# Keys' copies and differences over ten k tiles, the decay's chain in smaller pieces, the gate's two weight halves in one product

## The chip, the cores and the metric

The kernel runs on one core of one Trainium2 chip. The metric is the device time of one execution in microseconds, the median of three runs.

## The reference, cut to what matters

A decoder trunk of two post-norm layers on one sequence of 256 tokens, width 2048, in float32. Layer 0 mixes tokens by windowed attention, layer 1 by forgetting attention; after each comes a gated MLP (5632 wide) with a causal convolution of width 3. The change touches the forgetting attention alone:

```python
def forgetting_attention(x, w_qkvf, f_bias, w_o):
    proj = x @ w_qkvf                      # 2048 -> 3*2048 (q, k, v) and 32 gate columns
    q, k, v = ...                          # 32 heads of 64
    fz = proj[..., 3 * B_DIM:] + f_bias
    cum = jnp.cumsum(jax.nn.log_sigmoid(fz), axis=1)      # the decay, per head
    s = q @ k.T * SCALE + cum[query] - cum[key]           # causal
    return softmax(s) @ v, then @ w_o
```

## The kernel before

**Precision.** TensorE multiplies in a format that holds only part of a float32. Every operand is therefore split in a high half (ACT copies it, which rounds it) and a low half (VectorE subtracts the high half from the original), and every product is three matmuls: high by low, low by high, high by high. Activations stand in `xh` and `xl`, weights in `w_hi` and `w_lo`.

**Chunks and the ring.** A group is a product of all 256 tokens with 512 weight columns, summed over 16 k tiles of 128. Two k tiles of weights (512 KB) are a chunk. Chunks go through a ring of four slots: SyncE loads `raw` when the low half of the chunk four earlier is made (`low_ready`), ACT makes `w_hi` (`L553`) when the chunk four earlier has been used by TensorE (`chunks_used`), VectorE makes `w_lo` (`L848`), TensorE multiplies. ACT works three chunks ahead (`AHEAD`), VectorE two (`LOW_AHEAD`). In ACT's and VectorE's programs the generator `slots` interleaves this with other work: it yields k = 0 to 15, the caller puts its step for that k there, and the split of a chunk follows each even k:

```python
for k in range(nk):
    if k == nk - 2:
        split(b4, loc0 + k // 2 + AHEAD)      # VectorE: LOW_AHEAD
    yield k
    if k % 2 == 0 and k != nk - 2:
        split(b4, loc0 + k // 2 + AHEAD)
```

Each engine carries out its own program strictly in the written order. The same k on two engines doesn't mean the same time: each runs as far ahead as its waits let it.

**The forgetting layer.** `mixer_b` has four turns of three groups (queries, keys, values) for eight heads each, turn 0 written out and turns 1 to 3 as a loop. Queries and keys are computed turned (tokens along the columns), 12 matmuls of 256 columns for each k tile (`L1318`, `L1320`, `L1321`); values straight, 6 matmuls of 512 columns (`L1300` to `L1302`). Results stand in banks of PSUM that must be copied out:

- while the keys group is computed, the queries are copied (`query_high` on ACT, `L609`; `query_low` on VectorE, `L938`), for banks b = 0, 1 and halves of the rows h = 0, 1;
- while the values group is computed, the keys are copied (`key_high` on ACT, `L616`, two copies for each b and h; `key_low` on VectorE, `L949`, two differences for each). ACT raises `k_high` with h = 1 only; VectorE waits for it with h = 0 of the same bank;
- after the values group, VectorE and ACT copy the values (`vv`, `L1157` and `L715`), and TensorE's next group, which writes to the same banks, waits for these copies. In turns 1 to 3 and at the output projection's start ACT loads the table for Exp (`L526`) ahead of its copy.

The queries group of turns 1 to 3 has the attention of the heads before woven into it (`attention_slot`). In turn 0 there is none; there the gate is computed: a narrow product with 32 columns (`L1605` to `L1607`, 48 matmuls) between queries and keys, and then in `decay`, under the keys group, the logarithm of the sigmoid and the running sum (VectorE `L1129` to `L1147`, ACT `L733` Exp and `L736` Ln, each with a table load). TensorE transposes the sum for the queries (`L1615`), and GpSimd writes it to memory and loads it back spread over the partitions, twice 1 MB, to make the bias of eight heads; then it loads two rows of the norm's parameters and scales a piece of the residual with them.

Of the kernel before, what the change touches and what calls it, by code (L numbers as in the profile page):

```python
# [26 lines left out]
P = 128  # L27
# [63 lines left out]

LATE = KT - KT // GROUPS
OUT_DONE = 2 * KT - KT // GROUPS
WOVEN_OUT = [(i, k) for ks in (range(LATE), range(LATE, KT)) for i in range(2) for k in ks]
# [34 lines left out]
def trunk(nc, x, a_w_qkv, a_w_o, a_sinks, rel_bias, b_w_qkvf, b_f_bias, b_w_o,  # L129
          ffn_w_up, ffn_conv_w, ffn_conv_b, ffn_w_down, ln_g, ln_b, out):  # L130
    ctx = ExitStack()
    with ctx:
# [46 lines left out]
        with ExitStack() as mix:  # L179
# [4 lines left out]
            with ExitStack() as gating:  # L184
                wf = sb("wf", [P, KT, HEADS], FP32, gating)
                wf_hi = sb("wf_hi", [P, KT, HEADS], F32R, gating)
                wf_lo = sb("wf_lo", [P, KT, HEADS], F32R, gating)
            bias_hold = sb("bias_hold", [P, HG * SPAN], FP32, mix)
# [332 lines left out]
        def _(act):  # L521
# [186 lines left out]
            def mixer_b():  # L708
                def turn(n, b4, first=False, nk=KT):

                    if not first:
                        load_table(ACT.Exp)
                        act.wait_ge(pv_done, n * HG + (GROUPS - 1) * HG)
                        act.wait_ge(chunks_used, n * (3 * KC) + CH_B)
                        act.activation(vv[:, 1, :], bank(0, 1), ACT.Copy).then_inc(acc_free[0][1], 1)  # L715
                    for k in slots(b4, 0, nk):
                        if first:
                            if k % 2 == 0 and k // 2 + 2 < KC:
                                xt_evacuate(2, 0, 1, k // 2 + 2)
                            if k == 13:  # L720
                                act.wait_ge(wf_in, 32)
                                act.activation(wf_hi[:, :, :], wf[:, :, :], ACT.Copy).then_inc(wf_high, 1)
                            continue
                        attention_slot(k, (n + (GROUPS - 1)) * HG, (n + (GROUPS - 1)) * 2, (n - 1) * 4, False)
                    if nk > KT:
                        return
                    act.wait_ge(chunks_used, n * (3 * KC) + (CH_B + KC))
                    for k in slots(b4, KC):
                        if k < 4:
                            query_high(0, k // 2, k % 2, False)  # L730
                        if first and k == 7:
                            act.wait_ge(decay_abs, 1)
                            act.activation(fs[2][:, :], fs[1][:, :], ACT.Exp).then_inc(decay_exp, 1)  # L733
                        if first and k == 9:
                            act.wait_ge(decay_u, 1)
                            act.activation(fs[4][:, :], fs[3][:, :], ACT.Ln).then_inc(decay_ln, 1)  # L736
                    act.wait_ge(chunks_used, n * (3 * KC) + (CH_B + 2 * KC))
                    for k in slots(b4, 2 * KC):
                        if k < 4:
                            key_high(1, k // 2, k % 2)  # L740

                turn(0, CH_B // 4, first=True)
                with act.Fori(0, GROUPS - 1) as i:
                    own.enter(i, 1)
                    turn(i + 1, i * (3 * KC // 4) + (CH_B + 3 * KC) // 4)
                    own.leave(GROUPS - 1)
                turn(GROUPS, CH_O[1] // 4, nk=2 * KT)
# [85 lines left out]
        def _(dve):  # L833
# [287 lines left out]
            def decay(k):  # L1121
# [3 lines left out]
                z, nabs, e, u, lnu, d, zero, cum, ncum = fs  # L1125
                if k == 3:
                    dve.wait_ge(fz_done, 1)
                    dve.wait_ge(wf_in, 32)
                    own.link(dve.tensor_scalar(z[:, :], ps[0:HEADS, 6, 0:SEQ], fbc[:, 0:1], None, ALU.add))  # L1129
                    dve.scalar_tensor_tensor(nabs[:, :], z[:, :], -1.0, z[:, :], ALU.mult, ALU.min).then_inc(decay_abs, 1)  # L1130
                if k == 7:
                    dve.wait_ge(decay_exp, 1)
# [3 lines left out]
                    own.link(dve.tensor_scalar(zero[:, :], d[:, :], 0.0, None, ALU.is_equal))  # L1136
                    own.link(dve.tensor_tensor(d[:, :], d[:, :], zero[:, :], ALU.add))
                    own.link(dve.reciprocal(d[:, :], d[:, :]))
                    own.link(dve.tensor_tensor(d[:, :], d[:, :], e[:, :], ALU.mult))
                if k == 9:  # L1140
                    dve.wait_ge(decay_ln, 1)
                    own.link(dve.tensor_tensor(lnu[:, :], lnu[:, :], zero[:, :], ALU.add))
                    own.link(dve.tensor_tensor(d[:, :], lnu[:, :], d[:, :], ALU.mult))
                    own.link(dve.scalar_tensor_tensor(z[:, :], z[:, :], 0.0, d[:, :], ALU.min, ALU.subtract))
                    own.link(dve.memset(zero[:, :], 1.0))
                    own.link(dve.tensor_tensor_scan(cum[:, :], zero[:, :], z[:, :], 0.0, ALU.mult, ALU.add))
                    dve.tensor_scalar(ncum[:, :], cum[:, :], -1.0, None, ALU.mult).then_inc(cum_ready, 1)  # L1147
                if k == 13:
                    dve.wait_ge(cum_turned, 1)
                    dve.tensor_copy(cumq[:, :, :], ps[:, 7, 0:MT * HEADS].rearrange("p (m h) -> p m h", m=MT)).then_inc(cumq_ready, 1)  # L1150

            def mixer_b():
                def turn(n, b4, first=False, nk=KT):
# [4 lines left out]
                    for k in slots(b4, 0, nk, after_norm=first):  # L1158
                        if first:
                            xt_next(2, 0, 1, k)  # L1160
                            if k == 13:
                                dve.wait_ge(wf_high, 1)
                                dve.tensor_tensor(wf_lo[:, :, :], wf[:, :, :], wf_hi[:, :, :].bitcast(FP32), ALU.subtract).then_inc(wf_low, 1)
                            continue
# [5 lines left out]
                    for k in slots(b4, KC):  # L1170
                        if k < 4:
                            query_low(0, k // 2, k % 2, False, n * 2 + (2 * GROUPS + k // 2 + 1))
                        if first:
                            decay(k)
                    for k in slots(b4, 2 * KC):
                        if k < 4:
                            key_low(1, k // 2, k % 2, n * 2 + (2 + k // 2 + 1))

# [113 lines left out]
        def _(pe):  # L1292
# [289 lines left out]
            def mixer_b():  # L1582
# [11 lines left out]
                def turn(n, b4, first=False):  # L1594
# [5 lines left out]
                    if first:  # L1600

                        pe.wait_ge(wf_low, 1)
                        o = ps[0:HEADS, 6, 0:SEQ]
                        for k in range(KT):
                            pe.matmul(o, wf_lo[:, k, :], xh[:, k, :], start=(k == 0), stop=False)  # L1605
                            pe.matmul(o, wf_hi[:, k, :], xl[:, k, :], start=False, stop=False)
                            last = pe.matmul(o, wf_hi[:, k, :], xh[:, k, :], start=False, stop=(k == KT - 1))  # L1607
                        last.then_inc(fz_done, 1)
                    if not first:
                        narrow_product()  # L1610
                    for k in turned_group(1, n + t1, b4, KC):
                        if first and k == 12:
                            pe.wait_ge(cum_ready, 1)
# [95 lines left out]
```

## Time and profile before

| | |
|---|---|
| median of three runs | 2172.21 us (2171.49 to 2173.5) |
| the profiled execution | 2171.2 us, span 2169.4 us |
| TensorE matmul busy | 2143.6 us (99%) |
| VectorE busy | 1353.8 us (62%) |
| ACT busy | 1068.0 us (49%) |
| GpSimd busy | 214.8 us (10%) |
| mean granted TensorE clock | 0.999 |

Times in the trace are counted from the span's start. The forgetting layer's projections lie between 1002 and 1325 us. The values group begins at 1137.94 in turn 1. A busy TensorE is not TensorE at its peak, since matmuls are pipelined: the distance between the starts of two matmuls is the pace, and a longer distance is a pause.

### The profile page before, as it was taken

The page shows a single profiled execution, that of the slowest core. Times are in us where ns is not written, and L with a number is a line of the kernel's source. Part 1 is how long each engine was busy: PE and PEld are TensorE (multiplying, and loading weights), DVE is VectorE, ACT ScalarE, POOL GpSimd, SP SyncE. Part 2 cuts the span into 40 slices and gives each one's busy share as a digit, 9 for nine tenths or more (in the row PEclk, how much of TensorE's full clock was granted, in tenths as well). Part 3 has the DMA queues.
Part 4 walks back from the last instruction along what each step waited for, and adds up shares of the span by engine and source line. Part 5 has one row for each costly group of instructions (what it writes and reads, how often), then busy time and mean ns, then how long its engine had stood idle before and what let it go on. Part 6 is the DMA issues. An engine that isn't in the chain of part 4 may idle for free.

```text
span 2169.4 us, 41044 instructions
## 1 busy us (share of the span) xinstructions
PE 2143.6 (99%) x15304; PEld 1995.4 (92%) x15304; DVE 1353.8 (62%) x1865; ACT 1068.0 (49%) x1433; POOL 214.8 (10%) x211
## 2 busy tenths in 40 slices
PE   9999999999999999999899999999999999999998
PEld 8998899999999988888798898889999999988887
DVE  5676676666666644446766666676666666655554
ACT  4655465545555543335545545355555555544432
POOL 2000003210000000000330330002121000000000
PEclk9999999999999999999999999999999999999999
DMA  8554567666666656564655655556676666666663
GB/s 280 152 179 138 175 189 211 204 203 192 194 193 193 192 185 203 192 195 142 199 166 161 205 171 156 176 173 204 203 207 197 192 193 192 193 213 193 193 193 125
DMA packets 206604, 407.69 MB, mean 188 GB/s; under 512 B 12832, under 2 KB 13408, under 8 KB 206400
## 3 DMA queue, kind: packets, MB, share of 16 engines
q1 hardware_dynamic: 199680, 384.35, 58.3%
q0 software_dynamic: 5984, 20.74, 3.1%
q10 hardware_dynamic: 864, 1.57, 0.2%
q8 instruction: 49, 0.80, 0.1%
q14 instruction: 27, 0.22, 0.0%
HBM read 404.44 MB, written 2.18 MB: 187 GB/s over the span
## 4 chain that ended last, share of the span: by engine, by line
PE 93%; DVE 4%; issue 1%; ACT 1%; DMA 1%; DVEq 0%; ACTq 0%; SPq 0%
PE ps L1318 18%; PE ps L1321 18%; PE ps L1320 18%; PE ps L1300 11%; PE ps L1301 11%; PE ps L1302 11%; DVE w_lo L848 1%; PE ps L1505 1%; DMA raw<-in_b_w_qkvf_dram 1%; PE ps L1516 1%; PE ps L1517 1%; PE ps L1515 1%; PE ps L1497 0%; PE ps L1402 0%; DVE cg L903 0%
## 5 line engine op out<-in xcount | busy, mean ns | idle before, releaser
L848 DVE TENSOR_TENSOR w_lo<-raw,w_hi 128x1024 fp32r<-128x1024 f32 x725 | 905.5, 1255 | 599.2 <-ACT w_hi L553 596.3
L553 ACT ACTIVATE w_hi<-raw 128x1024 fp32r<-128x1024 f32 x725 | 768.1, 1060 | 919.0 <-PE ps L1321 492.1
L1318 PE MATMUL ps<-xh,w_lo 128*128 128x256 f32 x3572 | 996.8, 279 | 5.1 <-ACT vv L715 2.6
L1321 PE MATMUL ps<-xh,w_hi 128*128 128x256 f32 x3572 | 988.6, 277 | 0.0
L1320 PE MATMUL ps<-xl,w_hi 128*128 128x256 f32 x3572 | 988.5, 277 | 0.0
L1318 PEld LDWEIGHTS ps<-xh,w_lo 128*128 128x128 f32 x3572 | 672.0, 188 | 8.4 <-DVE xl L899 3.1
L1320 PEld LDWEIGHTS ps<-xl,w_hi 128*128 128x128 f32 x3572 | 671.9, 188 | 0.0
L1321 PEld LDWEIGHTS ps<-xh,w_hi 128*128 128x128 f32 x3572 | 671.8, 188 | 0.0
L1302 PE MATMUL ps<-w_hi,hid_h 128*128 128x512 f32 x704 | 273.9, 389 | 0.0
L1301 PE MATMUL ps<-w_hi,hid_l 128*128 128x512 f32 x704 | 273.9, 389 | 0.0
L1300 PE MATMUL ps<-w_lo,hid_h 128*128 128x512 f32 x704 | 273.9, 389 | 0.0
L1300 PEld LDWEIGHTS ps<-w_lo,hid_h 128*128 128x128 f32 x704 | 132.2, 188 | 27.6
L1301 PEld LDWEIGHTS ps<-w_hi,hid_l 128*128 128x128 f32 x704 | 132.2, 188 | 27.3
L1302 PEld LDWEIGHTS ps<-w_hi,hid_h 128*128 128x128 f32 x704 | 132.2, 188 | 27.2
L462 POOL COPY cw<-convcol 128x16 f32 (+1 forms) x40 | 39.6, 991 | 746.9 <-DVE cu L1193 415.3
L1300 PE MATMUL ps<-w_lo,oh 128*128 128x512 f32 x256 | 101.7, 397 | 0.0
L1302 PE MATMUL ps<-w_hi,oh 128*128 128x512 f32 x256 | 99.8, 390 | 0.0
L1301 PE MATMUL ps<-w_hi,ol 128*128 128x512 f32 x256 | 99.8, 390 | 0.0
L1193 DVE SCALAR_TENSOR_TENSOR cu<-ps,cw,cu 128x254 f32<-128x254 f32 (+1 forms) x176 | 76.6, 477 | 1.6
L1193 DVE SCALAR_TENSOR_TENSOR cg<-ps,cw,cg 128x254 f32<-128x254 f32 (+1 forms) x176 | 76.6, 477 | 1.6
L1300 PE MATMUL ps<-w_lo,xh 128*128 128x512 f32 x148 | 59.5, 402 | 8.5 <-DVE w_lo L848 8.4
L1302 PE MATMUL ps<-w_hi,xh 128*128 128x512 f32 x148 | 58.2, 393 | 0.0
(197 smaller groups left out, 1604.9 us busy)
## 6 DMA issues: line engine op xcount, KB each, us to landing
raw<-in_ffn_w_up_dram SPq DMA_DIRECT2D x352, 512.0 KB, 3.7
raw<-in_ffn_w_down_dram SPq DMA_DIRECT2D x176, 512.0 KB, 4.6
raw<-in_b_w_qkvf_dram SPq DMA_DIRECT2D x96, 512.0 KB, 4.2
raw<-in_a_w_qkv_dram SPq DMA_DIRECT2D x39, 512.0 KB, 4.7
raw<-in_a_w_o_dram SPq DMA_DIRECT2D x32, 512.0 KB, 4.6
raw<-in_b_w_o_dram SPq DMA_DIRECT2D x32, 512.0 KB, 4.7
bias<-rel_by_distance POOLq DMA_DIRECT2D x4, 1024.0 KB, 6.5
bias<-minus_cumulated_decay POOLq DMA_DIRECT2D x4, 1024.0 KB, 6.5
```

What stands on the lines that cost most here:

```text
L462: gp.tensor_copy(cw[:, h], convcol[:, l, :, bass.ds(n * 4 + h * FT, 4)]).then_inc(cw_ready, 1)
L553: act.activation(w_hi[:, loc % RING], raw[:, loc % RING], ACT.Copy).then_inc(high_ready, 1)
L848: dve.tensor_tensor(w_lo[:, s], raw[:, s], w_hi[:, s].bitcast(FP32), ALU.subtract).then_inc(low_ready, 1)
L1193: last = dve.scalar_tensor_tensor(dst[:, j, lag:SEQ], src, cw[:, h, tap, j:j + 1], dst[:, j, lag:SEQ], ALU.mult, ALU.add)
L1300: pe.matmul(o, lh[:, k, rows], w_lo[:, slot, k % 2, :], start=(k == 0), stop=False)
L1301: pe.matmul(o, ll[:, k, rows], w_hi[:, slot, k % 2, :], start=False, stop=False)
L1302: last = pe.matmul(o, lh[:, k, rows], w_hi[:, slot, k % 2, :], start=False, stop=(k == nk - 1))
L1318: pe.matmul(o, w_lo[:, slot, k % 2, cols], xh[:, k, :], start=(k == 0 and j % 2 == 0), stop=False, skip_group_check=True)
L1320: pe.matmul(o, w_hi[:, slot, k % 2, cols], xl[:, k, :], start=False, stop=False, skip_group_check=True)
L1321: last = pe.matmul(o, w_hi[:, slot, k % 2, cols], xh[:, k, :], start=False, stop=(k == KT - 1), skip_group_check=True)
L1505: last = pe.transpose(ps[:, PT_BANK, b * P:(b + 1) * P], prob[:, j % 4, b * P:(b + 1) * P], ident[:, :])
L1515: pe.matmul(o[0], pt[:, 0:P], vv[:, 0, cols], start=True, stop=True)
```

## The change

Five edits, all in `mixer_b`. The keys' four copies on ACT and four differences on VectorE stand at k = 0, 3, 6 and 9 of the values group instead of k = 0, 1, 2, 3. The queries' stand two at k = 0 and two at k = 1. The gate's weights are put side by side in one tile, high then low, so that one matmul with 64 columns multiplies both; there are two for each k tile, and VectorE adds the two halves of the result (this also adds the product of the low halves). The decay's pieces move to k = 1, 3, 5, 7, 9, ACT's Exp and Ln to k = 1 and 3, the transposes from k = 12 to 14 and the copy of the result from 13 to 15. The Exp table is loaded at k = 12 of the values group, ahead of its use in the next turn, instead of at the turn's start.

```diff
--- before.py
+++ after.py
@@ -90,6 +90,7 @@
 
 
 LATE = KT - KT // GROUPS
+KEY_STEPS = {0: (0, 0), 3: (0, 1), 6: (1, 0), 9: (1, 1)}
 OUT_DONE = 2 * KT - KT // GROUPS
 WOVEN_OUT = [(i, k) for ks in (range(LATE), range(LATE, KT)) for i in range(2) for k in ks]
 
@@ -183,8 +184,7 @@
                 bias = sb("bias", [P, HG, SPAN], FP32, attending)
             with ExitStack() as gating:
                 wf = sb("wf", [P, KT, HEADS], FP32, gating)
-                wf_hi = sb("wf_hi", [P, KT, HEADS], F32R, gating)
-                wf_lo = sb("wf_lo", [P, KT, HEADS], F32R, gating)
+                wf2 = sb("wf2", [P, KT, 2, HEADS], F32R, gating)
             bias_hold = sb("bias_hold", [P, HG * SPAN], FP32, mix)
 
             q2 = sb("q2", [P, 4, 2, SEQ], F32R, mix)
@@ -709,7 +709,6 @@
                 def turn(n, b4, first=False, nk=KT):
 
                     if not first:
-                        load_table(ACT.Exp)
                         act.wait_ge(pv_done, n * HG + (GROUPS - 1) * HG)
                         act.wait_ge(chunks_used, n * (3 * KC) + CH_B)
                         act.activation(vv[:, 1, :], bank(0, 1), ACT.Copy).then_inc(acc_free[0][1], 1)
@@ -719,25 +718,28 @@
                                 xt_evacuate(2, 0, 1, k // 2 + 2)
                             if k == 13:
                                 act.wait_ge(wf_in, 32)
-                                act.activation(wf_hi[:, :, :], wf[:, :, :], ACT.Copy).then_inc(wf_high, 1)
+                                act.activation(wf2[:, :, 0, :], wf[:, :, :], ACT.Copy).then_inc(wf_high, 1)
                             continue
                         attention_slot(k, (n + (GROUPS - 1)) * HG, (n + (GROUPS - 1)) * 2, (n - 1) * 4, False)
                     if nk > KT:
                         return
                     act.wait_ge(chunks_used, n * (3 * KC) + (CH_B + KC))
                     for k in slots(b4, KC):
-                        if k < 4:
-                            query_high(0, k // 2, k % 2, False)
-                        if first and k == 7:
+                        if k < 2:
+                            for h in range(2):
+                                query_high(0, k, h, False)
+                        if first and k == 1:
                             act.wait_ge(decay_abs, 1)
                             act.activation(fs[2][:, :], fs[1][:, :], ACT.Exp).then_inc(decay_exp, 1)
-                        if first and k == 9:
+                        if first and k == 3:
                             act.wait_ge(decay_u, 1)
                             act.activation(fs[4][:, :], fs[3][:, :], ACT.Ln).then_inc(decay_ln, 1)
                     act.wait_ge(chunks_used, n * (3 * KC) + (CH_B + 2 * KC))
                     for k in slots(b4, 2 * KC):
-                        if k < 4:
-                            key_high(1, k // 2, k % 2)
+                        if k in KEY_STEPS:
+                            key_high(1, *KEY_STEPS[k])
+                        if k == 12:
+                            load_table(ACT.Exp)
 
                 turn(0, CH_B // 4, first=True)
                 with act.Fori(0, GROUPS - 1) as i:
@@ -1123,29 +1125,32 @@
 
 
                 z, nabs, e, u, lnu, d, zero, cum, ncum = fs
-                if k == 3:
+                if k == 1:
                     dve.wait_ge(fz_done, 1)
                     dve.wait_ge(wf_in, 32)
                     own.link(dve.tensor_scalar(z[:, :], ps[0:HEADS, 6, 0:SEQ], fbc[:, 0:1], None, ALU.add))
+                    own.link(dve.tensor_tensor(z[:, :], z[:, :], ps[HEADS:2 * HEADS, 6, 0:SEQ], ALU.add))
                     dve.scalar_tensor_tensor(nabs[:, :], z[:, :], -1.0, z[:, :], ALU.mult, ALU.min).then_inc(decay_abs, 1)
-                if k == 7:
+                if k == 3:
                     dve.wait_ge(decay_exp, 1)
                     dve.tensor_scalar(u[:, :], e[:, :], 1.0, None, ALU.add).then_inc(decay_u, 1)
                     dve.wait_ge(decay_u, 1)
                     own.link(dve.tensor_scalar(d[:, :], u[:, :], -1.0, None, ALU.add))
                     own.link(dve.tensor_scalar(zero[:, :], d[:, :], 0.0, None, ALU.is_equal))
                     own.link(dve.tensor_tensor(d[:, :], d[:, :], zero[:, :], ALU.add))
+                if k == 5:
                     own.link(dve.reciprocal(d[:, :], d[:, :]))
                     own.link(dve.tensor_tensor(d[:, :], d[:, :], e[:, :], ALU.mult))
-                if k == 9:
+                if k == 7:
                     dve.wait_ge(decay_ln, 1)
                     own.link(dve.tensor_tensor(lnu[:, :], lnu[:, :], zero[:, :], ALU.add))
                     own.link(dve.tensor_tensor(d[:, :], lnu[:, :], d[:, :], ALU.mult))
                     own.link(dve.scalar_tensor_tensor(z[:, :], z[:, :], 0.0, d[:, :], ALU.min, ALU.subtract))
+                if k == 9:
                     own.link(dve.memset(zero[:, :], 1.0))
                     own.link(dve.tensor_tensor_scan(cum[:, :], zero[:, :], z[:, :], 0.0, ALU.mult, ALU.add))
                     dve.tensor_scalar(ncum[:, :], cum[:, :], -1.0, None, ALU.mult).then_inc(cum_ready, 1)
-                if k == 13:
+                if k == 15:
                     dve.wait_ge(cum_turned, 1)
                     dve.tensor_copy(cumq[:, :, :], ps[:, 7, 0:MT * HEADS].rearrange("p (m h) -> p m h", m=MT)).then_inc(cumq_ready, 1)
 
@@ -1160,7 +1165,7 @@
                             xt_next(2, 0, 1, k)
                             if k == 13:
                                 dve.wait_ge(wf_high, 1)
-                                dve.tensor_tensor(wf_lo[:, :, :], wf[:, :, :], wf_hi[:, :, :].bitcast(FP32), ALU.subtract).then_inc(wf_low, 1)
+                                dve.tensor_tensor(wf2[:, :, 1, :], wf[:, :, :], wf2[:, :, 0, :].bitcast(FP32), ALU.subtract).then_inc(wf_low, 1)
                             continue
                         attention_slot(k, (n + (GROUPS - 1)) * HG, (n + (GROUPS - 1)) * 2, (n - 1) * 4, n + (GROUPS - 1), False)
                         if k == OUT_DONE:
@@ -1168,13 +1173,15 @@
                     if nk > KT:
                         return
                     for k in slots(b4, KC):
-                        if k < 4:
-                            query_low(0, k // 2, k % 2, False, n * 2 + (2 * GROUPS + k // 2 + 1))
+                        if k < 2:
+                            for h in range(2):
+                                query_low(0, k, h, False, n * 2 + (2 * GROUPS + k + 1))
                         if first:
                             decay(k)
                     for k in slots(b4, 2 * KC):
-                        if k < 4:
-                            key_low(1, k // 2, k % 2, n * 2 + (2 + k // 2 + 1))
+                        if k in KEY_STEPS:
+                            b, h = KEY_STEPS[k]
+                            key_low(1, b, h, n * 2 + (2 + b + 1))
 
                 turn(0, CH_B // 4, first=True)
                 with dve.Fori(0, GROUPS - 1) as i:
@@ -1600,16 +1607,16 @@
                     if first:
 
                         pe.wait_ge(wf_low, 1)
-                        o = ps[0:HEADS, 6, 0:SEQ]
+                        o = ps[0:2 * HEADS, 6, 0:SEQ]
                         for k in range(KT):
-                            pe.matmul(o, wf_lo[:, k, :], xh[:, k, :], start=(k == 0), stop=False)
-                            pe.matmul(o, wf_hi[:, k, :], xl[:, k, :], start=False, stop=False)
-                            last = pe.matmul(o, wf_hi[:, k, :], xh[:, k, :], start=False, stop=(k == KT - 1))
+                            both = wf2[:, k, :, :].rearrange("p c h -> p (c h)")
+                            pe.matmul(o, both, xl[:, k, :], start=(k == 0), stop=False)
+                            last = pe.matmul(o, both, xh[:, k, :], start=False, stop=(k == KT - 1))
                         last.then_inc(fz_done, 1)
                     if not first:
                         narrow_product()
                     for k in turned_group(1, n + t1, b4, KC):
-                        if first and k == 12:
+                        if first and k == 14:
                             pe.wait_ge(cum_ready, 1)
                             for m in range(MT):
                                 last = pe.transpose(ps[:, 7, m * HEADS:(m + 1) * HEADS], fs[7][:, m * P:(m + 1) * P],
```

## Rows read from the trace of the kernel before

**Rows 1.** The page, busy time by engine, and the granted clock in 40 slices.
```profile
PE 2143.6 (99%) x15304; PEld 1995.4 (92%) x15304; DVE 1353.8 (62%) x1865; ACT 1068.0 (49%) x1433; POOL 214.8 (10%) x211
...
PEclk9999999999999999999999999999999999999999
```
**Rows 2.** The page, the chain that ended last, shares by engine.
```profile
PE 93%; DVE 4%; issue 1%; ACT 1%; DMA 1%; DVEq 0%; ACTq 0%; SPq 0%
```
**Rows 3.** TensorE's waits over the whole run: us in total, times, longest.
```profile
PE ps L1300 <- DVE w_lo L848: 8.4, 9, 2.2
PE ps L1318 <- ACT vv L715: 2.6, 1, 2.6
```
**Rows 4.** The same view, 1100 to 1330 us alone.
```profile
PE ps L1300 <- DVE w_lo L848: 5.3, 6, 1.1
```
**Rows 5.** Timeline, TensorE, turn 1's values: start us, us, line, idle before.
```profile
1137.94 0.39 PE L1300 MATMUL ps<-w_lo,xh 128*128 128x512 f32 x1
...
1143.20 0.40 PE L1302 MATMUL ps<-w_hi,xh 128*128 128x512 f32 x1
1144.33 0.50 PE L1300 MATMUL ps<-w_lo,xh 128*128 128x512 f32 x1 [0.74 <-DVE w_lo L848]
...
1146.98 0.39 PE L1302 MATMUL ps<-w_hi,xh 128*128 128x512 f32 x1
1148.42 0.50 PE L1300 MATMUL ps<-w_lo,xh 128*128 128x512 f32 x1 [1.05 <-DVE w_lo L848]
```
**Rows 6.** Timeline, ACT, turn 1's values.
```profile
1138.14 1.20 ACT L616 ACTIVATE k_hi<-ps 64x512 fp32r<-64x512 f32 x2 [0.83 <-PE ps L1321]
```
**Rows 7.** Timeline, VectorE, turn 0's values (first row) and turn 1's.
```profile
1059.07 2.41 DVE L848 TENSOR_TENSOR w_lo<-raw,w_hi 128x1024 fp32r<-128x1024 f32 x1
...
1141.66 1.38 DVE L949 TENSOR_TENSOR k_lo<-ps,k_hi 64x512 fp32r<-64x512 f32 x2 [3.14 <-ACT k_hi L616]
1143.05 1.23 DVE L848 TENSOR_TENSOR w_lo<-raw,w_hi 128x1024 fp32r<-128x1024 f32 x1
```
**Rows 8.** Timeline, TensorE, turn 1's keys at the second chunk's end.
```profile
1121.05 0.28 PE L1321 MATMUL ps<-xh,w_hi 128*128 128x256 f32 x1
1121.37 0.38 PE L1318 MATMUL ps<-xh,w_lo 128*128 128x256 f32 x1
```
**Rows 9.** Timeline, TensorE, first narrow matmul and first one after them.
```profile
1021.22 0.28 PE L1605 MATMUL ps<-xh,wf_lo 128*32 128x256 f32 x1
...
1026.66 0.28 PE L1318 MATMUL ps<-xh,w_lo 128*128 128x256 f32 x1
```
**Rows 10.** Timelines, VectorE's first and last decay operation, TensorE before the transposes.
```profile
1034.03 0.47 DVE L1129 TENSOR_SCALAR fs<-ps,fbc 32x256 f32<-32x256 f32 x1
...
1045.09 0.28 DVE L1147 TENSOR_SCALAR fs<-fs 32x256 f32<-32x256 f32 x1
...
1044.23 0.28 PE L1321 MATMUL ps<-xh,w_hi 128*128 128x256 f32 x1
1045.43 0.31 PE L1615 MATMUL ps<-ident,fs 32*128 32x32 f32 x2 [0.92 <-DVE fs L1147]
```
**Rows 11.** Timelines of turn 0, ACT at the values group's start and end.
```profile
1050.07 1.19 ACT L616 ACTIVATE k_hi<-ps 64x512 fp32r<-64x512 f32 x2 [1.60 <-PE ps L1321]
...
1076.40 1.06 ACT L553 ACTIVATE w_hi<-raw 128x1024 fp32r<-128x1024 f32 x1 [4.07 <-DMA raw<-in_b_w_qkvf_dram]
1077.48 1.28 ACT L526 ACT_TABLE_LOAD   x1
...
1079.18 0.60 ACT L715 ACTIVATE vv<-ps 128x512 f32<-128x512 f32 x1 [0.20 <-ACT warm L526]
```
**Rows 12.** Windows: stretch, its length, busy by engine, PEclk, DMA share, GB/s.
```profile
1077.00:1079.80 2.80, 0.19 (x2) 0.00 (x0) 1.23 (x1) 2.57 (x5) 1.93 (x1) 1.00 1.00 385
...
1081.00:1084.40 3.40, 3.40 (x19) 3.40 (x18) 1.26 (x1) 1.06 (x1) 3.32 (x3) 0.50 0.58 172
...
1058.90:1061.50 2.60, 0.40 (x2) 0.00 (x0) 2.56 (x2) 1.14 (x2) 2.60 (x2) 1.00 0.21 79
```

## The prediction

> **What bounds the kernel now.** I read the page first: TensorE is busy for 99% of the span at its full clock but for one dip, VectorE for 62% (the one dip of the clock, below, is too short for a digit of the page), and the chain that ended last is 93% TensorE with 4% VectorE in it [rows 1, 2]. So a change counts for what it does to TensorE's matmuls or to the few places where TensorE stands still. The view of waits names those places: over the whole run the largest entry is `w_lo` (the low halves of a weight chunk), 8.4 us in nine waits, and six of them, 5.3 us, lie in turns 1 to 3 of the forgetting layer's loop [rows 3, 4]. The timelines of turn 1 then show how such a wait comes about, and this is the pattern on which the forecast rests.
>
> Call T the start of the values group, 1137.94 in turn 1. Four k tiles run without a pause: their last matmul starts at 1143.20, so two chunks last 5.49 us (0.23 a matmul, 2.74 a chunk), and chunk 2 should start at T+5.49. It starts at 1144.33, 0.90 late; chunk 3 starts at 1148.42, 1.44 after the matmul before it and so 1.21 late; and the first matmul after each pause takes 0.50 instead of 0.39, another 0.11 each. Turn 1 loses 2.3 us [rows 5]. The cause stands on the two other engines. ACT makes the keys' high copies, VectorE their differences (`L949`), and VectorE's `w_lo` of chunk 2 stands behind the first pair of differences in its queue: differences 1141.66, `w_lo` 1143.05, and the product starts as it ends [rows 6, 7]. The differences start when ACT has copied both halves of bank 0, because `k_high` goes up with h = 1 alone.
>
> **The change, part by part.** *Keys' copies.* What matters is not that the four steps lie further apart but that VectorE keeps its first step at k = 0 and there waits for ACT's second step, now at k = 3. Between them ACT has the high half of chunk 4 in its queue, which waits until TensorE has used up chunk 0. ACT sees the end of a product 0.2 us after TensorE starts the next one (1138.14 against 1137.94), a pair of key copies takes 1.20, a pair of differences 1.38, a low half 1.23 [rows 5 to 7], a high half 1.06 [rows 11]. From T: chunk 0 used at 2.74, seen at 2.95, high half of chunk 4 until 4.0, key copies (bank 0, h = 1) until 5.2, differences until 6.6, `w_lo` of chunk 2 until 7.9. It is due at 5.49, so TensorE pauses 2.45 and pays 0.11 to restart. The same rule applied to the kernel before (0.2 + 1.2 + 1.06 + 1.2 for the copies, 1.38, 1.23) gives 6.3, against the 6.4 of the row, so the rule carries. The second bank repeats it: VectorE arrives at k = 6 and waits for ACT's step at k = 9, behind the high half of chunk 7, which waits for chunk 3. If chunk 3 is used at X, ACT sees it at X+0.2, then 1.06 + 1.2 + 1.38 + 1.23 make X+5.1 to X+5.2; VectorE has got to chunk 4 only, so chunk 5, due at X+2.74, is 2.45 late again. A turn then loses 2 x (2.45+0.11) = 5.1 where it lost 2.3: +2.8. Turns 2 and 3 show the same pauses as turn 1 (0.9 and 1.2; 0.8 and 1.2), so +8.3 for the three. The spreading does take the old 0.9 and 1.2 away, since only one pair of differences stands between two low halves. What would hide the new wait is slack in the low halves; VectorE is two chunks ahead, and the 5.49 is that slack, already spent.
>
> *Queries' copies.* Both halves of a bank together let the differences start after 1.2 us instead of behind a high half, and the pause of 0.2 us before chunk 2 of the keys (1121.05 to 1121.37, where 0.11 is the pace) should go [rows 8]. It stands twice, in turns 1 and 3: -0.4, between -0.4 and 0.
>
> *Gate.* The narrow product is 48 matmuls from 1021.22 to 1026.66, 0.113 each [rows 9]. It becomes 32 with 64 columns of weights. That is the pace of the matmuls with 128 columns around it too, so 64 cost no more: 16 x 0.113 = -1.8. One more addition on VectorE (0.4) lies under the keys group.
>
> *Decay.* Before, TensorE stands 0.92 before the two transposes at k = 12 (1044.23 to 1045.43, start to start 1.2 where 0.11 is the pace) [rows 10]. From its first operation at 1034.03 to its last at 1045.37 the chain took 11.3, two table loads on ACT and three low halves included. Now it starts at k = 1, about 3 us after the keys' start, and would end at 14 to 15 even at its old length; the transposes follow the product of k = 14, at 20.4 (15 tiles of 1.36): -1.0. Two or three of its operations between two low halves are at most 2.2 us in the 2.74 of a chunk less 1.23, on top of two chunks in hand, so no low half comes past its due time. GpSimd's bias loads come a little later relative to T; turn 1's attention, their user, is a group away.
>
> *Exp table.* In turns 1 to 3 the table load lies on ACT under the last VectorE copy, and the 0.3 us of TensorE at the turn's end is VectorE's `vv`; nothing to gain. In turn 0 ACT splits a late chunk until 1077.5, loads the table for 1.28 and ends `vv` at 1079.8, and TensorE waits 2.6 [rows 3, 11]. The load now hides at k = 12.
>
> *Turn 0 as a whole.* Before, the keys' copies start at 1050.07, so T is 1049.87; TensorE goes on at 1079.83 with 0.7 us of the next group done: 29.3 us [rows 11]. After: 8 chunks 21.9, two pauses 5.1, `vv` 0.3, and what GpSimd costs VectorE: a low half at 1059.07, in a stretch where GpSimd was busy throughout, took 2.41 instead of 1.23 [rows 7, 12]; one or two such on the path are 0 to 2.1, I take 1.0. That is 28.3 to 28.4, -0.9. If the scale's transfers delay chunk 10 as before, `vv` is still late and it is up to +0.6; if GpSimd is out of the way, -1.9.
>
> *The clock.* After the 2.6 us at 1077 the granted clock falls to 0.50 for 3.4 us (half speed, 1.2 GHz, with 19 matmuls begun); after the pause at 1058.9, whose idle part is 2.2 us, it stays at 1.00 [rows 12]. Such a dip costs between 1.3 (19 matmuls are 2.1 us of work at 0.113) and 1.7 (half of 3.4), I take 1.6. The dip of turn 0 goes with its `vv` wait: -1.6. But the timetable above has eight pauses of 2.45 us, with some 2.3 idle in each: between those two rows. One of two was followed by a dip, so I take four of eight: +6.4, with both ends, 0 and +12.8, kept for the range. Against this speaks the Trainium skill, TensorE: Matmul & The Clock Gate, section HAM oscillation, which warns only of idle gaps longer than any in this timetable; by it no pause would cost a dip and the sum would be 6.4 less. The dip after 2.6 us in this trace does not agree with it.
>
> **Sum.** 8.3 - 0.4 - 1.8 - 1.0 - 0.9 - 1.6 = +2.6, with the dips +9.0. The profiled execution took 2171.2 (span 2169.4); the median of the runs is 2172.2, 1.0 more. Forecast: 2180.2 in the profiled execution's terms, 2181.2 for the median.
>
> **Rivals.**
> (1) *The clock holds.* All pauses come, no dip: +2.6, 2174.8. For it: the pause at 1058.9. Against it: the dip at 1081, after a pause 0.3 longer than these. It is also what that page of the Trainium skill would have. A measurement of this kernel tells about 0.2% (4.3 us) from no change, so this is mostly "same".
> (2) *Every pause is followed by a dip*: +15.4, 2187.6. For it: 2.3 idle is nearer to 2.2 than to 2.6, but the dips need not go by length alone.
> (3) *Faster: VectorE doesn't wait for ACT's step.* Place: the wait for `k_high` in front of `L949` at k = 0 and 6. It decides at T+2.7: if ACT has the second half of the bank copied by then, differences (1.4) and low half (1.2) still fit before 5.49 and nothing is late. Then the pauses of four turns go: -7.0 in turns 1 to 3, turn 0 goes from 29.3 to 21.9 and 0.3, -7.1, and -4.8 for the rest: -18.9, 2153.3. Against it: ACT's queue order puts a wait for TensorE at 2.95 ahead of that copy.
> (4) *Turn 0 keeps its late chunk* and its dip: +0.6 in place of -0.9 and no -1.6, so +3.1 on any of the above; it widens the range.
>
> **How the numbers follow.** Forecast with some dips (two to six of eight) 0.62; clock holds or one dip 0.13; seven or eight dips or turn 0 late as well 0.17; faster 0.04; something between (pauses half as long) 0.04. The likeliest gives 2181.2. The range must take in no-dip sums with rounding and most of rival 2: from +3 to +15, 2175.2 to 2187.2. Slower by over 0.2% (above 2176.5): 0.62 + 0.17 + 0.04 = 0.83; same, the clock that holds, 0.13; faster 0.04.
>
> **What would show it.** In the profile after: TensorE's matmuls of `L1302` followed by a gap of about 2.7 us start to start at chunks 2 and 5 of each values group, ended by `w_lo`; VectorE idle before its key differences for about 5 us, twice a turn, released by ACT; ACT's table load at k = 12; 32 narrow matmuls in 3.6 us; no wait before the transposes; stretches of 3.4 us at a granted clock of 0.50 after some of the pauses. The prediction is wrong if VectorE's waits at k = 0 and 6 are short, or if the clock stays at 1.00 or falls every time.

## The result: slower by half a per cent

The changed kernel takes 2181.85 us (median of 6 runs, 2180.99 to 2184.49) against 2171.85 for the kernel before (6 runs, 2164.06 to 2173.62): a ratio of 1.0052, 95% interval 1.0041 to 1.0063. The forecast was 2181.2. The profiled execution took 2181.54, 10.3 more than the one of before, with a span of 2179.7.

The page after, busy time by engine, answers to [rows 1]:

```profile
PE 2146.0 (98%) x15288; PEld 1996.7 (92%) x15288; DVE 1353.8 (62%) x1866; ACT 1065.7 (49%) x1431; POOL 214.3 (10%) x211
```

TensorE is busy 2.4 us more although it has 16 matmuls fewer (some of them run at half clock, as shown below), and VectorE and ACT do what they did. So the ten microseconds are no added work; TensorE's waits, which answer to [rows 3], show most of them:

```profile
PE ps L1307 <- DVE w_lo L850: 19.6, 9, 3.0
```

The wait for low halves has grown from 8.4 to 19.6 us; the wait for ACT's `vv` and the one before the transposes are gone from the list. Turn 1's values group, TensorE's timeline, answers to [rows 5] (`L1307` to `L1309` are the old `L1300` to `L1302`):

```profile
1139.83 0.39 PE L1309 MATMUL ps<-w_hi,xh 128*128 128x512 f32 x1
1142.45 0.51 PE L1307 MATMUL ps<-w_lo,xh 128*128 128x512 f32 x1 [2.23 <-DVE w_lo L850]
...
1150.60 0.40 PE L1309 MATMUL ps<-w_hi,xh 128*128 128x512 f32 x1
1154.04 0.50 PE L1307 MATMUL ps<-w_lo,xh 128*128 128x512 f32 x1 [3.04 <-DVE w_lo L850]
```

Start to start the two pauses are 2.62 and 3.44 where 0.23 is the pace, so 2.4 and 3.2 us. ACT and VectorE in the same stretch, in place of [rows 6, 7]:

```profile
1134.66 1.20 ACT L616 ACTIVATE k_hi<-ps 64x512 fp32r<-64x512 f32 x2 [1.46 <-PE ps L1328]
1135.87 1.06 ACT L553 ACTIVATE w_hi<-raw 128x1024 fp32r<-128x1024 f32 x1
1137.46 1.06 ACT L553 ACTIVATE w_hi<-raw 128x1024 fp32r<-128x1024 f32 x1 [0.54 <-PE ps L1309]
1138.55 1.20 ACT L616 ACTIVATE k_hi<-ps 64x512 fp32r<-64x512 f32 x2
...
1149.05 1.06 ACT L553 ACTIVATE w_hi<-raw 128x1024 fp32r<-128x1024 f32 x1 [1.56 <-DMA raw<-in_b_w_qkvf_dram]
1150.13 1.20 ACT L616 ACTIVATE k_hi<-ps 64x512 fp32r<-64x512 f32 x2
...
1139.78 1.38 DVE L951 TENSOR_TENSOR k_lo<-ps,k_hi 64x512 fp32r<-64x512 f32 x2 [5.25 <-ACT k_hi L616]
1141.18 2.36 DVE L850 TENSOR_TENSOR w_lo<-raw,w_hi 128x1024 fp32r<-128x1024 f32 x2
```

Read from top to bottom this is the timetable of the forecast: ACT copies the first half of bank 0, makes a high half, waits for TensorE to use up chunk 0 (0.54), makes the next high half, and only then, at 1138.55, copies the second half. VectorE has stood idle for 5.25 us; its differences start at 1139.78, the low half that TensorE needs at 1141.18 (the row holds two), and TensorE goes on at 1142.45. The second pause of this turn is 0.8 longer than the others because the high half of chunk 7 also waited for its transfer (1149.05); in the two further profiles of this kernel, below, that pause is 0.0 and 0.3 us longer than the others.

The last part of the price stands in the windows (stretch, length, busy by engine, PEclk, DMA share, GB/s): after some pauses the granted clock falls to 0.50, that is 1.2 GHz, for 3.4 us.

```profile
1151.00:1154.00 3.00, 0.00 (x0) 0.00 (x0) 2.61 (x4) 1.48 (x3) 0.00 (x0) 1.00 0.00 0
1154.10:1157.50 3.40, 3.40 (x15) 2.81 (x16) 3.32 (x4) 0.00 (x0) 0.00 (x0) 1.00 0.61 173
1224.80:1227.40 2.60, 0.38 (x2) 0.00 (x0) 2.57 (x4) 2.15 (x3) 0.00 (x0) 1.00 0.00 0
1227.50:1230.90 3.40, 3.40 (x8) 2.72 (x9) 3.33 (x4) 0.00 (x0) 0.00 (x0) 0.50 0.61 177
```

The first pair is the long pause of turn 1, three idle microseconds and then 15 matmuls in 3.4 us at full clock. The second pair is a shorter pause of turn 2, and 8 matmuls in the same time.

### The profile page after: what moved, and what is told of

The parts are those of the page before. It is cut to its first block, busy times and chain, and to the rows that moved or that the text cites. A ratio compares the mean times of both kernels' runs of the same rounds, so it can differ in the third digit from the quotient of the medians.

```text
span 2179.7 us, 41011 instructions
## 1 busy us (share of the span) xinstructions
PE 2146.0 (98%) x15288; PEld 1996.7 (92%) x15288; DVE 1353.8 (62%) x1866; ACT 1065.7 (49%) x1431; POOL 214.3 (10%) x211
## 4 chain that ended last, share of the span: by engine, by line
PE 93%; DVE 3%; ACT 1%; issue 1%; DMA 1%; DVEq 0%; ACTq 0%; SPq 0%
PE ps L1325 19%; PE ps L1328 18%; PE ps L1327 18%; PE ps L1307 11%; PE ps L1309 11%; PE ps L1308 11%; DVE w_lo L850 1%; PE ps L1512 1%; PE ps L1524 1%; PE ps L1523 1%; DMA raw<-in_b_w_qkvf_dram 1%; PE ps L1522 0%; PE ps L1504 0%; ACT k_hi L616 0%; PE ps L1409 0%
## 5 line engine op out<-in xcount | busy, mean ns | idle before, releaser
L1309 PE MATMUL ps<-w_hi,hid_h 128*128 128x512 f32 x704 | 273.9, 389 | 0.0
L1307 PE MATMUL ps<-w_lo,hid_h 128*128 128x512 f32 x704 | 273.9, 389 | 0.0
L1307 PEld LDWEIGHTS ps<-w_lo,hid_h 128*128 128x128 f32 x704 | 132.1, 188 | 27.5
L1309 PEld LDWEIGHTS ps<-w_hi,hid_h 128*128 128x128 f32 x704 | 132.1, 188 | 27.2
L1307 PE MATMUL ps<-w_lo,oh 128*128 128x512 f32 x256 | 101.7, 397 | 0.0
L1309 PE MATMUL ps<-w_hi,oh 128*128 128x512 f32 x256 | 99.8, 390 | 0.0
L1307 PE MATMUL ps<-w_lo,xh 128*128 128x512 f32 x148 | 62.2, 420 | 19.6 <-DVE w_lo L850 19.6
L1309 PE MATMUL ps<-w_hi,xh 128*128 128x512 f32 x148 | 60.7, 410 | 0.0
```

What stands on the lines that cost most here:

```text
L1307: pe.matmul(o, lh[:, k, rows], w_lo[:, slot, k % 2, :], start=(k == 0), stop=False)
L1309: last = pe.matmul(o, lh[:, k, rows], w_hi[:, slot, k % 2, :], start=False, stop=(k == nk - 1))
```

## The experiments

The theory: VectorE's first key step of each bank waits for ACT's second one, which now stands behind a wait for TensorE; the eight pauses of about 2.5 us that follow, and the dips of the clock after some of them, are the whole loss, and the other edits gain a little. The rivals: one of the other edits costs; or the spread itself does, by making low halves and so transfers late; or the dips are no part of it.

### One edit undone, one edit alone

The key steps back, all else as changed:

```diff
-                        if k in KEY_STEPS:
-                            key_high(1, *KEY_STEPS[k])
+                        if k < 4:
+                            key_high(1, k // 2, k % 2)
...
-                        if k in KEY_STEPS:
-                            b, h = KEY_STEPS[k]
-                            key_low(1, b, h, n * 2 + (2 + b + 1))
+                        if k < 4:
+                            key_low(1, k // 2, k % 2, n * 2 + (2 + k // 2 + 1))
```

> The changed kernel with the keys' copies and differences back at k = 0 to 3; the other four edits stay. If the keys' new places are what costs, the eight pauses of about 2.4 us and their dips go, the old small pauses (0.9 and 1.2 a turn) come back, and what is left of the change is its gain: 0.4 + 1.8 + 1.0 + the late values copy of turn 0 (about 2.6) and its dip (1.6), 7.4 us less than before: about 2164.5. If the keys' places are not the cause and one of the other edits costs, the time stays near 2182.

Measured: 2165.14 us (10 runs, 2164.44 to 2166.42), ratio to before 0.9977 (0.9967 to 0.9986). The rest of the change gains some 6.5 us where 7.4 were expected (TensorE still waits 1.8 us for the values copy of turn 0), and the keys' places cost it all and 10 more. In its trace the pauses of turns 1 to 3 are again 1.0 to 1.1 and 1.4 us start to start, as in [rows 5]. Its runs lie within 2 us of each other, where those of the kernel before spread over 9.

The opposite, the kernel before with the `KEY_STEPS` lines and nothing else:

> The kernel before with the keys' steps at k = 0, 3, 6, 9 and nothing else. If the keys' new places are the cause, +8.3 for turns 1 to 3, 0 to +3 for turn 0 (its pauses grow, its table load stays in the way) and half of eight pauses followed by a dip of 1.6, one dip lost: 2172 + 8.3 + 1.5 + 4.8 = 2187, between 2182 and 2193. If they are not the cause, 2172.

Measured: 2187.10 (4 runs, 2181.64 to 2188.88), ratio 1.0082 (1.0065 to 1.0099), as expected. TensorE's waits in the profiled execution, which with 2181.64 is the shortest of the four (no trace shows what the other three paid beyond it):

```profile
PE ps L1302 <- DVE w_lo L849: 18.8, 9, 2.6
```

So the keys' places alone make the loss, and none of the other edits is needed for it. What these two runs don't tell is whether the spread costs or the order of the waits.

### Spread kept, wait mended

```diff
                 for to in range(2):
                     ins = act.activation(k2_hi[...], key_bank(...), ACT.Copy)
-                if h == 1:
-                    ins.then_inc(k_high, 1)
+                ins.then_inc(k_high, 1)
...
-                if h == 0:
-                    dve.wait_ge(k_high, count)
+                dve.wait_ge(k_high, count)
...
-                            key_low(1, b, h, n * 2 + (2 + b + 1))
+                            key_low(1, b, h, n * 4 + (2 + 2 * b + h + 1))
```

> The changed kernel with every step where the change put it; ACT raises k_high after each half of a bank instead of after the second one, and VectorE waits for its own half alone. If VectorE's wait at k = 0 and 6 for ACT's step at k = 3 and 9 is the whole cause, the low half of chunk 2 is ready at T+4.0 and that of chunk 5 three us before its time: no pause in any values group, no dip, and 20.5 + 0.8 + 6.4 us less: about 2154. If the spread itself costs (later low halves, so later transfers into the ring), pauses remain and the time stays above 2165.

Measured: 2152.78 us (4 runs, 2151.97 to 2154.26), ratio 0.9919 (0.9903 to 0.9936), 29 us less than the changed kernel with every step in the same place. VectorE in turn 1's values group, and below it two windows over the values groups of turns 0 and 1:

```profile
1129.32 1.38 DVE L949 TENSOR_TENSOR k_lo<-ps,k_hi 64x512 fp32r<-64x512 f32 x2 [1.54 <-ACT k_hi L616]
1130.71 2.36 DVE L849 TENSOR_TENSOR w_lo<-raw,w_hi 128x1024 fp32r<-128x1024 f32 x2
...
1135.91 1.38 DVE L949 TENSOR_TENSOR k_lo<-ps,k_hi 64x512 fp32r<-64x512 f32 x2
```
```profile
1044.00:1069.00 25.00, 25.00 (x127) 21.10 (x127) 19.25 (x18) 15.78 (x19) 14.42 (x9) 1.00 0.74 236
1127.00:1149.00 22.00, 22.00 (x102) 18.20 (x102) 15.82 (x17) 13.32 (x17) 1.92 (x1) 1.00 0.69 215
```

The 5.25 us of VectorE's idleness are 1.54, its low halves come in pairs ahead of their time, and TensorE is busy for 22.00 of 22.00 us. The rival of the spread falls: the steps are as far apart as before, and nothing pauses.

The same reached by order alone, the semaphore as it was (the steps lie closer together here than in the change, so it speaks for the wait and not on the spread):

```diff
-KEY_STEPS = {0: (0, 0), 3: (0, 1), 6: (1, 0), 9: (1, 1)}
+HIGH_STEPS = {0: (0, 0), 1: (0, 1), 3: (1, 0), 5: (1, 1)}
+LOW_STEPS = {1: (0, 0), 3: (0, 1), 5: (1, 0), 7: (1, 1)}
```

> The changed kernel with the semaphore as it was, but ACT's key steps at k = 0, 1, 3, 5 and VectorE's at k = 1, 3, 5, 7, so that a bank's second half is copied ahead of the next wait for TensorE and VectorE makes the low half of chunk 2 before its first key step. If what costs is where VectorE's wait stands against ACT's queue, there is no pause: low half of chunk 3 at T+6.3 (due 8.2), of chunk 5 at T+11.5 (due 13.7), about 2153, as with each half told. If a bank's differences need a signal for each half, pauses stay and it is above 2165.

Measured: 2152.87 (4 runs, 2152.13 to 2155.09), ratio 0.9913 (0.9897 to 0.9930). Two different cures of one wait give the same time to 0.1 us.

### Pauses kept, idleness taken away

```diff
+                    def fill(c):
+                        if c in (2, 5):
+                            if first and c == 2:
+                                pe.wait_ge(cumq_ready, 1)
+                            keep_clock(2.1)
-                    for k in group(0, n * 2 + (t0 + 1), b4, 2 * KC, xh, xl, tile0=v_tile0):
+                    for k in group(0, n * 2 + (t0 + 1), b4, 2 * KC, xh, xl, before=fill, tile0=v_tile0):
```

> The changed kernel; TensorE does five matmuls on the identity (2.1 us) ahead of its wait for chunk 2 and for chunk 5 of each values group, so that the pauses stay and only their idleness goes. If four dips of 1.6 us are part of the price, the granted clock stays at 1.00 in these turns and the time falls by 6.4 to about 2175.5. If the dips cost nothing beyond the pauses, it stays at 2182; if the added matmuls delay the chunks, it rises.

Measured: 2176.42 (10 runs, 2173.42 to 2179.62), ratio to before 1.0025 (1.0015 to 1.0034), 5.4 less than the changed kernel; expected were 6.4. The fill writes to the PSUM bank in which the transposed sum lies, hence the wait for `cumq_ready`; the trace lists it as ten matmuls of 256 columns, 2.32 us in all, where the text above has five. The filled pauses of turn 1 in the windows:

```profile
1139.00:1144.00 5.00, 4.92 (x22) 3.84 (x21) 4.91 (x6) 1.75 (x3) 0.00 (x0) 1.00 0.42 112
1150.00:1155.00 5.00, 4.88 (x22) 3.78 (x21) 4.91 (x6) 0.42 (x2) 0.00 (x0) 1.00 0.43 127
```

The useful work stops about as long as before (22.3 us in eight pauses, start to start, against 22.5), but the clock stays at 1.00 in all four turns. So about 5.4 us of the changed kernel's time are the price of idleness, on top of the pauses themselves; the medians of two kernels whose runs spread over 3.5 and 6 us don't give it more closely. The two profiled executions differ by 6.9.

### Which pauses are followed by a dip

> The changed kernel as it is, profiled once more. Its first profile has eight pauses and dips of the granted clock after four of them: after the second one of turn 0, both of turn 2 and the first of turn 3. If a pause's length alone decides, the same four are followed by a dip again. If it is a matter of where the pause falls on a clock of the chip's own, the eight pauses are the same to 0.1 us and another set of them, three to six, is followed by a dip, and the time moves by 1.6 us for each.

> The same once more: the same eight pauses, and by length alone the same four dips, otherwise a third set of three to six.

> The kernel before, profiled once more. Its runs lie between 2165 and 2174. Its two long idle stretches are those of 2.2 us (turn 0's second pause) and 2.6 us (the late values copy). By length alone a dip follows the second one again and not the first, 2171; otherwise it may follow both, either or none, with 2172.5, 2171 or 2169.5.

Measured: 2182.42, 2184.38 and 2171.05 us. Six of the eight pauses are the same in all three profiles of the changed kernel within 0.1 us (2.6 to 2.7 start to start); turn 0's second one is 3.1, 2.7 and 2.7, turn 1's second one 3.4, 2.7 and 2.9. Followed by a dip were four pauses in the first profile, six in the second, five in the third: 15 of 24. Turn 1's second pause in the second and in the third profile:

```profile
1152.50:1154.90 2.40, 0.23 (x2) 0.00 (x0) 2.37 (x4) 1.15 (x2) 0.00 (x0) 1.00 0.00 0
1155.00:1158.40 3.40, 3.39 (x15) 2.81 (x16) 3.33 (x4) 0.00 (x0) 0.00 (x0) 1.00 0.62 170
```
```profile
1152.80:1155.30 2.50, 0.06 (x1) 0.00 (x0) 2.47 (x4) 1.15 (x2) 0.00 (x0) 1.00 0.00 0
1156.50:1159.80 3.30, 3.30 (x9) 2.56 (x8) 3.24 (x4) 0.00 (x0) 0.00 (x0) 0.50 0.93 285
```

A pause is thus followed by a dip in one execution and not in the next, and the longest one of all, 3.0 us idle at 1151 in the first profile, by none. Length alone doesn't decide.

What one dip costs can be read off by laying the first profile beside the second, over the same 36 matmuls between the two pauses of turn 1, without a dip and with one:

```profile
1142.40:1150.60 8.20, 8.14 (x36) 6.68 (x36) 3.75 (x5) 2.72 (x4) 0.00 (x0) 1.00 0.65 194
1142.60:1152.40 9.80, 9.78 (x36) 7.84 (x36) 3.78 (x5) 3.35 (x5) 0.00 (x0) 0.83 0.54 162
```

From the first of them to the last, start to start, they take 8.15 us (1142.45 to 1150.60) and 9.73 (1142.62 to 1152.35): 1.6 us for a dip, as taken in the forecast.

In the second profile of the kernel before, the pause in turn 0 with 2.6 us idle was followed by 6.8 us at half clock, and the wait for the late values copy was 0.4 us instead of 2.6; this was not among the cases expected, and the time, 2171.05, is the same. The three times of the changed kernel don't follow the count of dips (4, 6, 5) closely either. One other reason shows in the traces: matmuls of 256 columns start every 0.113 us in some stretches and every 0.118 in others, and the same stretch can have the one pace in one execution and the other in the next (ahead of the gate's product 0.118 in the first profile, 0.113 in the second), which would be 0.9 us over the 192 matmuls of a whole group. Why is open.

### The smaller edits

The gate's weights side by side in the kernel before, nothing moved (the diff is the gate's part of the change):

> The kernel before with the gate's weights side by side and one more addition on VectorE, nothing moved. If 64 columns cost TensorE what 32 do, 16 matmuls of 0.113 go: the narrow product takes 3.6 instead of 5.4 us, the wait before the transposes stays 0.9 and grows by at most the addition's 0.4: 2170. If a wider load of weights costs, the narrow product takes more than 3.8 and less is gained.

Measured: 2168.13 (10 runs, 2162.49 to 2170.87), ratio 0.9983 (0.9972 to 0.9995). The last narrow matmuls and the first wide one:

```profile
1024.51 0.28 PE L1606 MATMUL ps<-xl,wf 128*64 128x256 f32 x1
1024.63 0.28 PE L1607 MATMUL ps<-xh,wf 128*64 128x256 f32 x1
1024.75 0.28 PE L1318 MATMUL ps<-xh,w_lo 128*128 128x256 f32 x1
```

The product starts at 1020.95 and takes 3.80 us, 0.119 a matmul instead of 0.113: 1.6 us gained rather than 1.8. This is not the price of 64 columns: the wide matmuls just ahead of it have the slower pace too, 0.118, in this run as in the first profile of the changed kernel. In the changed kernel's second profile the wide ones ahead have 0.113, and so have the 32 narrow ones, 3.62 us from the first row to the last:

```profile
1020.52 0.28 PE L1613 MATMUL ps<-xl,wf 128*64 128x256 f32 x1
...
1024.14 0.28 PE L1325 MATMUL ps<-xh,w_lo 128*128 128x256 f32 x1
```

So 64 columns cost what 128 do, as forecast, and the gate gives 1.8 where the pace is the same. The rest of the 3.5 us of the medians is not the gate's by any row.

The table load alone:

```diff
                     if not first:
-                        load_table(ACT.Exp)
...
                         if k < 4:
                             key_high(1, k // 2, k % 2)
+                        if k == 12:
+                            load_table(ACT.Exp)
```

> The kernel before with the Exp table loaded at k = 12 of the values group instead of at the next turn's start. Turn 0: ACT's values copy comes 1.5 us earlier after the late chunk, TensorE waits 1.1 instead of 2.6, and after so short an idle stretch the clock should hold, another 1.6: between 1.5 and 3.1 less, 2169. Turns 1 to 3: nothing, VectorE's copy ends last there. If the table load at k = 12 delays a chunk, pauses appear at chunk 9 and it is no faster than before.

Measured: 2167.68 (10 runs, 2165.40 to 2169.31), ratio 0.9982 (0.9973 to 0.9992). ACT at the end of turn 0's values group, where [rows 11] has the load between the late chunk and the copy:

```profile
1076.09 1.06 ACT L553 ACTIVATE w_hi<-raw 128x1024 fp32r<-128x1024 f32 x1 [4.13 <-DMA raw<-in_b_w_qkvf_dram]
1077.17 0.60 ACT L714 ACTIVATE vv<-ps 128x512 f32<-128x512 f32 x1
```

TensorE waits 1.1 us there instead of 2.6, and the profile has no dip in this layer: 1.5 and 1.6, 3.1 of the 4.0 us between the medians; the rest is in no row read here. The load alone doesn't decide whether the wait occurs: with the load in its old place it is absent in the profile of the keys' steps alone, and 0.4 us in the second one of the kernel before.

The queries' edit gained nothing. In the changed kernel the pause in turns 1 and 3 is what it was (0.33 start to start for 0.11). VectorE and GpSimd in turn 1 of the changed kernel:

```profile
1114.47 2.86 DVE L850 TENSOR_TENSOR w_lo<-raw,w_hi 128x1024 fp32r<-128x1024 f32 x1
...
1114.35 1.90 POOL L496 TENSOR_TENSOR bias<-bias,cumq 128x1024 f32<-128x1024 f32 x1
```

The low half is issued 0.12 us behind the start of the first of GpSimd's two additions and takes 2.86 instead of 1.23; it ends 1.08 after that addition's end (1116.25). In the kernel before it was issued 0.36 behind (1118.70 against 1118.34) and took 2.61: both end 3.0 us after the addition's start. Test, on top of the mended kernel:

```diff
-                        if k < 2:
+                        if k in (1, 3):
                             for h in range(2):
-                                query_low(0, k, h, False, n * 2 + (2 * GROUPS + k + 1))
+                                query_low(0, k // 2, h, False, n * 2 + (2 * GROUPS + k // 2 + 1))
```

> The kernel with each half told, and VectorE's query differences at k = 1 and 3 instead of 0 and 1. The pause of 0.2 us in turns 1 and 3 stayed after the change because the low half of chunk 2 starts just behind an addition of GpSimd and takes 2.85 instead of 1.23. If it has to wait for that addition to end, issuing it 1.4 us earlier, ahead of the addition, brings it to at most 1.6 and the pause goes: 0.4 us less, 2152.4, to be seen in the trace rather than in the time. If it is slow for another reason, it stays near 2.8 and the pause stays.

Measured: 2151.75 (4 runs, 2150.58 to 2152.99), ratio 0.9906 (0.9889 to 0.9922).

```profile
1105.95 1.33 DVE L849 TENSOR_TENSOR w_lo<-raw,w_hi 128x1024 fp32r<-128x1024 f32 x1
1107.32 1.39 DVE L939 SCALAR_TENSOR_TENSOR q<-ps,q 64x512 fp32r<-64x512 f32 x2
...
1104.12 2.08 POOL L496 TENSOR_TENSOR bias<-bias,cumq 128x1024 f32<-128x1024 f32 x1 [6.67 <-DMA bias<-minus_cumulated_decay]
```

Issued before the query differences the low half takes 1.33, and both pauses are gone. It still begins under an addition, the one before those two, but under its last 0.25 us (until 1106.20), and ends 1.08 after it, as above. The 1.0 us between the medians is within the spread of the runs; the trace accounts for 0.4. This is the fastest version: 20 us less than the kernel before, 30 less than the change.

## Why the prediction was right, point by point

- **Keys' copies, turns 1 to 3**: forecast +8.3. The pauses are 2.4 and 3.2, 2.4 and 2.4, 2.4 and 2.4, with six restarts of 0.11 some 16.0; before 7.0. So +9.0; the 0.7 too little is the late transfer of turn 1, which the timetable left out. In the second profile, where that transfer is not late, the six pauses and restarts make 15.3: +8.3, the forecast. That the pauses come from VectorE's wait for `k_high` is shown twice, by the finer signal and by the new order.
- **Queries**: forecast -0.4, measured 0. The term was mis-sized: the low half does start 0.24 earlier against GpSimd's addition, but takes 0.25 longer, because its end is set by that addition (3.0 us after its start in both kernels). The forecast had the low half depend on nothing but its place in VectorE's queue; that was the step that failed here.
- **Gate**: forecast -1.8, measured -1.6 in the first profile, at the slower pace that the matmuls around had, and -1.8 in the second.
- **Decay**: forecast -1.0. From the keys' first matmul (1024.66) to the values' (1046.88, 0.2 before ACT's first key copy) it is 22.2 us after, 23.2 before, and no wait stands before the transposes: -1.0. It was not run alone.
- **Turn 0's values with the table load**: forecast 28.3 to 28.4 us and no late copy. Measured 30.0 from 1046.88 to 1076.87 with one dip in it, which leaves 28.4. That the late copy stays away is the table load's doing is not shown (see its run).
- **The clock**: forecast four dips of eight and the old one gone, +4.8 in all; the profile has exactly four. That was luck within a range: the other two profiles have six and five, and 5 of 8 is the better figure. The price of a dip, 1.6, is measured. The price of idleness, measured by filling it, is 5.4 us for the median, against 6.4 forecast; five dips of 1.6 would be 8.0, and this gap is open.

The terms as measured, 9.0 + 0 - 1.6 - 1.0 - 0.9 + 4.8, make 10.3, which is the difference of the two profiled executions; forecast were 9.0. That the forecast of the median, 2181.2, lies only 0.7 below the measured one is in part luck: it added 1.0 for a median above the profiled execution, and here the median is 0.3 above it. Rivals 1 (the clock holds), 2 (every pause has its dip) and 3 (faster, no wait) are refuted for the change, and rival 4's long wait for a late values copy in turn 0 came in none of the three profiles (0.6 us at most); rival 3's sum, 2153.3, is what the kernel takes once the wait is mended (2152.8), so the eight pauses were all that stood between.

## What to carry to other kernels

When steps of two engines are spread over a common numbering, move the producer's signals with them: a consumer that waits at its first step for the producer's last now waits for all that stands between, here a wait for TensorE. Write a timetable of the two queues from T for one period; it gave six of the eight pauses here to within 0.1 us. And where TensorE pauses for 2.4 us as here, count between 0.7 us (5.4 by filling eight pauses) and 1.0 (5 of 8 dips of 1.6) for each pause beyond its length.

## What the runs showed of the hardware

- Idle stretches of 2.2 to 3.0 us were followed by 3.4 us at half clock in 15 of 24 cases, the same stretch in one execution and not in another; one such dip cost 1.6 us. The Trainium skill (TensorE: Matmul & The Clock Gate, HAM oscillation) warns only of longer gaps; these runs don't agree with it.
- A low half on VectorE (two inputs from SBUF) beside an addition on GpSimd took up to 2.9 us instead of 1.2, and 1.33 when issued 0.25 us before the addition's end; all of these ended 1.1 us after the addition. The Trainium skill (SBUF — State Buffer, Summary: rules for kernel authors) says that a VectorE instruction with two SBUF inputs and a GpSimd one that reads SBUF contend, and that the one issued second waits until the first has finished; these times fit that.
